# Input units of the first block in a new order, as filling of the recurrent chain and of attention; one activation table for exp and ln in the second block

## What is computed

```python
def first_block(x, ...):                 # per layer
    p_swa, p_rwkv, p_fox, p_dsa, p_gate = split_cols(x @ w_in, IN_GROUPS)
    o = swa_branch(...), rwkv7_branch(...), fox_branch(...), dsa_branch(...)
    gates = sigmoid(p_gate.reshape(B, S, 4, 1024) + gate_bias)
    x = layer_norm(DN_ALPHA * x + (sum_i gates[i] * (o[i] @ w_rows[i])) @ w_out, ...)
    x = layer_norm(DN_ALPHA * x + (swiglu(x) if layer == 0 else moe_ffn(x)), ...)
```

## Time and profile before

| | before |
|---|---|
| median of 3 runs | 2380.99 us (2380.73 to 2382.38) |
| the profiled execution | 2379.34 us, its span 2377.6 us |
| PE / DVE / ACT / POOL busy | 2177.4 / 654.0 / 435.2 / 81.7 us |
| mean granted clock of PE | 0.954 |
| read from HBM | 417.90 MB, 176 GB/s over the span |

### The profile page before, as it was taken

The page is one execution under the profiler, slowest core; times in us unless marked ns, Lnnn a source line. Parts: engine busy times, 40 slices in busy tenths (PEclk is TensorE's granted clock), DMA queues, the critical chain, the costliest instruction groups (busy, mean ns, idle before and its releaser), DMA issues.

```text
span 2377.6 us, 34188 instructions
## 1 busy us (share of the span) xinstructions
PE 2177.4 (92%) x14812; PEld 1566.2 (66%) x14812; DVE 654.0 (28%) x1567; ACT 435.2 (18%) x897; POOL 81.7 (3%) x180
## 2 busy tenths in 40 slices
PE   8999679999989897788899999988899998889998
PEld 7878457677768686565554365367577766757775
DVE  0051643424320333643200000033433332341001
ACT  0031131100010121230000000046610004661000
POOL 2000000001000000001000000000001010000000
PEclk9999869999999899788899999999999999999999
DMA  8333203488744232112899999953368854232442
GB/s 252 110 107 108 98 18 115 160 265 292 251 148 138 89 107 98 53 63 91 265 345 333 360 346 310 375 185 104 110 209 269 296 185 135 91 105 91 159 159 88
DMA packets 329659, 421.25 MB, mean 177 GB/s; under 512 B 21015, under 2 KB 277989, under 8 KB 329509
## 3 DMA queue, kind: packets, MB, share of 16 engines
q1 hardware_dynamic: 308304, 352.96, 46.0%
q0 software_dynamic: 13408, 50.66, 6.3%
q10 hardware_dynamic: 7796, 15.43, 1.9%
HBM read 417.90 MB, written 1.05 MB: 176 GB/s over the span
## 4 chain that ended last, share of the span: by engine, by line
PE 46%; ACT 4%; DVE 4%; issue 1%; DMA 1%; ACTq 0%; DVEq 0%
PE psum L1219 11%; PE psum L1336 10%; PE psum L1237 6%; PE psum L1396 5%; PE psum L1226 5%; PE psum L1635 2%; PE psum L1878 1%; PE psum L1255 1%; PE psum L1464 1%; PE psum L1325 1%; PE psum L1409 1%; ACT arena L996 1%; PE psum L1155 1%; ACT L967 1%; PE psum L1618 1%
## 5 line engine op out<-in xcount | busy, mean ns | idle before, releaser
L1219 PE MATMUL psum<-xT,ring 128*128 128x256 f32 (+1 forms) x3584 | 801.4, 384 | 7.0 <-DVEq L417 2.9
L1219 PEld LDWEIGHTS psum<-xT,ring 128*128 128x128 f32 (+1 forms) x3584 | 678.5, 190 | 129.5 <-issue 23.0
L1237 PE MATMUL psum<-ring,arena 128*128 128x512 f32 x528 | 232.2, 593 | 0.0
L1226 PE MATMUL psum<-ring,xT 128*128 128x256 f32 (+3 forms) x1024 | 216.8, 370 | 15.5 <-DVE arena L2268 8.1
L1226 PEld LDWEIGHTS psum<-ring,xT 128*128 128x128 f32 x1024 | 185.7, 199 | 44.6 <-DVE arena L2268 9.3
L1237 PEld LDWEIGHTS psum<-ring,arena 128*128 128x128 f32 x528 | 100.0, 190 | 114.2 <-issue 111.9
L2063 DVE TENSOR_TENSOR arena<-arena,psum 128x512 f32<-128x512 f32 x33 | 22.7, 688 | 410.7 <-PE psum L1219 235.0
L2052 DVE SCALAR_TENSOR_TENSOR arena<-arena,cond 128x256 f32<-128x256 f32 x336 | 135.0, 480 | 0.0
L1336 PE MATMUL psum<-ring,arena 128*32 128x256 f32 x2304 | 126.8, 379 | 0.7 <-DVE arena L2135 0.7
L657 ACT ACTIVATE arena<-psum 128x512 f32<-128x512 f32 x33 | 19.7, 597 | 578.2 <-PE psum L1219 571.9
L1336 PEld LDWEIGHTS psum<-ring,arena 128*32 128x32 f32 x2304 | 74.7, 110 | 51.2 <-issue 3.4
(11 more groups left out here) (392 smaller groups left out, 1972.8 us busy)
## 6 DMA issues: line engine op xcount, KB each, us to landing
ring<-in_w_in SPq DMA_DIRECT2D x80, 1024.0 KB, 5.3
ring<-in_exp_w SPq DMA_DIRECT2D x312, 256.0 KB, 6.1
arena<-in_w_mod POOLq DMA_DIRECT2D x48, 1024.0 KB, 9.4
ring<-in_ffn_w SPq DMA_DIRECT2D x33, 1024.0 KB, 6.8
arena<-in_exp_w SPq DMA_DIRECT2D x120, 256.0 KB, 7.1
ring<-in_w_gate SPq DMA_DIRECT2D x22, 1024.0 KB, 7.6
ring<-in_w_up SPq DMA_DIRECT2D x22, 1024.0 KB, 10.0
ring<-in_w_down SPq DMA_DIRECT2D x22, 1024.0 KB, 5.1
```

The lines of the kernel that those rows point to most:

```text
L1219: ins = pe.matmul(dst, w[:, k * 256 + c0:k * 256 + c0 + m], act_t[:, k, :], start=(k == 0), stop=(k == KT - 1))
L1226: ins = pe.matmul(dst, act_t[:, k, t * P:t * P + P], w[:, k * 256 + c0:k * 256 + c0 + n], start=(k == 0), stop=(k == KT - 1))
L1237: ins = pe.matmul(psum[:, 4 + 2 * t + h, :], gT[:, s % 3, f * 256 + t * P:f * 256 + t * P + P], w2[:, f * D + h * 512:f * D + h * 512 + 51 ...
```

## The change

The units of a layer are loaded and multiplied in the order 3, 4, 5, 6 (`RWKV_IN`), then 10, 11, 12, 7, 8, 9, 0, 1, 2 (`FILL_IN`), then the gates. Only the first four are done ahead of the chain, into banks 4, 5, 0 and 1. The other nine and the 16 gates are one list of 25 fills, handed out by `fill` at the places where `gates` stood and at some more: three (layer 1: two) before the up-projections instead of two, one behind the variance matmul, five (six) instead of two with the picking, five instead of one in attention. ACT copies all of them. Unit 11 is packed anew, so that one channel tile gives both kinds of keys and one token tile per half the values, the index weights and the forget logits, which two transposes turn later. The barrier behind the input stage is gone; DVE waits for the parameters and for ACT's copy of unit 5 by themselves. `load_params` waits for unit 5 in slot 2 where it waited for unit 2, the same third load. In the second block one table set that holds exp and ln is loaded ahead of its use in each layer, and each root gets a Newton step of three small DVE operations (`newton`).

```diff
+RWKV_IN = (3, 4, 5, 6)
+FILL_IN = (10, 11, 12, 7, 8, 9, 0, 1, 2)
+FILLS = len(FILL_IN) + 16
...
-        def in_bank(i):
-            return (4 + i) % 8
-
-        def in_copied(ready, l, i):
-            return ready("act" if i in (0, 1, 3, 5, 7, 9, 10) else "dve", "in", l, i)
+        RAW_BANK = {3: 4, 4: 5, 5: 0, 6: 1}
+        PAR_BANK = 2
...
-                for i, c in enumerate(units1):
+                for i in RWKV_IN + FILL_IN:
+                    c = units1[i]
                     if c is None:
-                        yield ("in", l, i), [(0, 128, w[:, :, IN_DSA + 256:IN_DSA + 384]),
-                                             (128, 68, w[:, :, IN_DSA + 640:IN_DSA + 708]),
+                        yield ("in", l, i), [(0, 64, w[:, :, IN_DSA + 256:IN_DSA + 320]),
+                                             (64, 64, w[:, :, IN_DSA + 640:IN_DSA + 704]),
+                                             (128, 64, w[:, :, IN_DSA + 320:IN_DSA + 384]),
+                                             (192, 4, w[:, :, IN_DSA + 704:IN_DSA + 708]),
...
+            def fill(l, n, banks):
 
                 for _ in range(n):
-                    j = gates_done[0] % 16
-                    gates_done[0] += 1
-                    cp, b = gate_place(j)
-                    act.wait_ge(*ready("pe_job", "gate", l, j))
-                    for i in range(2):
-                        c = 2 * cp + i
-                        step(act.activation(zb[:, b, c, :], psum[:, banks[j % len(banks)], i * 256:i * 256 + 256],
-                                            ACT.Identity, bias=prm(l, "gate_b", b * KT + c)), "zb", l, j)
-
-            gates_done = [0]
+                    j = filled[0] % FILLS
+                    filled[0] += 1
+                    bank = psum[:, banks[j % len(banks)], :]
+                    act.wait_ge(*ready("pe_job", "fill", l, j))
+                    if j >= len(FILL_IN):
+                        cp, b = gate_place(j - len(FILL_IN))
+                        for i in range(2):
+                            c = 2 * cp + i
+                            step(act.activation(zb[:, b, c, :], bank[:, i * 256:i * 256 + 256],
+                                                ACT.Identity, bias=prm(l, "gate_b", b * KT + c)), "filled", l, j)
...
+                    elif FILL_IN[j] == 2:
+                        for g in range(2):
+                            for h in range(2):
+                                step(act.copy(swa_k[hb(h), g, :], bank[hb(g), 0:256]))
+                        step(act.copy(swa_v[:], two(bank[:, 256:512])), "filled", l, j)
+                    elif FILL_IN[j] == 11:
+                        for h in range(2):
+                            step(act.copy(dsa_k[hb(h), :], bank[0:HD, 0:256]))
+                            step(act.copy(dsa_ki[hb(h), :], bank[HD:P, 0:256]))
+                        token = bank[:, 256:400].rearrange("p (t c) -> p t c", t=NT)
+                        step(act.copy(dsa_v[:], token[:, :, 0:HD]))
+                        step(act.activation(dsa_wi[:], token[:, :, HD:HD + 4], ACT.Copy, scale=SCALE * 0.5))
+                        step(act.copy(forget, token[:, :, HD + 4:HD + 8]), "filled", l, j)
+                    else:
+                        dst = {0: swa_q[:, 0:2, :], 1: swa_q[:, 2:4, :], 7: fox_q, 8: fox_k, 9: fox_v,
+                               10: dsa_q, 12: dsa_qi}[FILL_IN[j]]
+                        step(act.copy(dst[:], two(bank)), "filled", l, j)
...
-                act.wait_ge(*ready("slot2", "unit", "in", 0, 2))
+                act.wait_ge(*ready("slot2", "unit", "in", 0, 5))
...
-                for i, dst in ((0, swa_q[:, 0:2, :]), (1, swa_q[:, 2:4, :]), (3, raw[:, 0:2, 1:]),
-                               (5, raw[:, 4:6, 1:]), (7, fox_q[:]), (9, fox_v[:]), (10, dsa_q[:])):
+                for i, dst in ((3, raw[:, 0:2, 1:]), (5, raw[:, 4:6, 1:])):
                     act.wait_ge(*ready("pe_job", "in", l, i))
-                    step(act.copy(dst, psum[:, in_bank(i), :].rearrange("p (a b) -> p a b", a=2)), "in", l, i)
+                    step(act.copy(dst, two(psum[:, RAW_BANK[i], :])), "in", l, i)
+                fill(l, 1, (6,))
...
+                act.preload_act_table_set("natural_log_exp_and_others")
...
+            def fill(l, n, banks):
 
                 for _ in range(n):
-                    j = gates_done[0] % 16
-                    gates_done[0] += 1
+                    j = filled[0] % FILLS
+                    filled[0] += 1
                     bank = banks[j % len(banks)]
-                    if bank in gate_in:
-
-                        pe.wait_ge(*ready("act", "zb", l, gate_in[bank]))
-                    w = unit("gate", l, *gate_place(j))
-                    for i in range(2):
-                        ins = channel_tile(psum[:, bank, i * 256:i * 256 + 256], w, i * P, P)
-                    job(ins, "gate", l, j)
-                    used("gate", l, *gate_place(j))
-                    gate_in[bank] = j
-
-            gates_done, gate_in = [0], {}
+                    if bank in fill_in:
+                        pe.wait_ge(*ready("act", "filled", l, fill_in[bank]))
+                    key = ("in", l, FILL_IN[j]) if j < len(FILL_IN) else ("gate", l, *gate_place(j - len(FILL_IN)))
+                    w = unit(*key)
+                    if key == ("in", l, 9):
+                        for t in range(NT):
+                            ins = token_tile(psum[:, bank, t * 256:t * 256 + 256], w, 0, 256, t)
+                    elif key in (("in", l, 2), ("in", l, 11)):
+                        n_tok = P if key[2] == 2 else HD + 8
+                        channel_tile(psum[:, bank, 0:256], w, 0, P)
+                        for t in range(NT):
+                            ins = token_tile(psum[:, bank, 256 + t * n_tok:256 + (t + 1) * n_tok], w, P, n_tok, t)
+                    else:
+                        for i in range(2):
+                            ins = channel_tile(psum[:, bank, i * 256:i * 256 + 256], w, i * P, P)
+                    job(ins, "fill", l, j)
+                    used(*key)
+                    fill_in[bank] = j
+
+            filled, fill_in = [0], {}
...
+                for i in RWKV_IN[2:4]:
...
+                fill_in.clear()
+                fill(l, 1, (6,))
                 if l == 0:
-                    pe.wait_ge(*in_copied(ready, l, 6))
                     pe.wait_ge(S.sem("param"), N_PARAM_LOADS * 16)
                     for i in range(DEPTH):
-                        ins = pe.transpose(psum[:, in_bank(14), i * P:i * P + N_PAR], par_rows[0:N_PAR, i, :],
+                        ins = pe.transpose(psum[:, PAR_BANK, i * P:i * P + N_PAR], par_rows[0:N_PAR, i, :],
                                            ident[0:N_PAR, 0:N_PAR])
                     job(ins, "par")
                 else:
-                    pe.wait_ge(*in_copied(ready, l, 6))
-                    turn_mod(0, in_bank(14))
-                barrier()
-
-
-                gate_in.clear()
-                gates(l, G[0], (6,))
+                    turn_mod(0, PAR_BANK)
+                fill(l, G[0][l] - 1, (6,))
                 pe.wait_ge(*ready("act", "tanh", l))
...
                 pe.wait_ge(*ready("dve", "y_sq", l))
                 ins = pe.matmul(psum[:, 5, :], block_ones[:], sq[:], start=True, stop=True)
                 job(ins, "var", l)
-                gates(l, G[9], (6,))
+                fill(l, G[9], (6,))
                 barrier()
 
-                gate_in.clear()
+                fill_in.clear()
+                for t in range(NT):
+                    ins = pe.transpose(psum[0:4, 2, t * P:t * P + P], forget[:, t, :], ident[:])
+                job(ins, "forget", l)
...
-                gates(l, G[6], (0, 1))
+                fill(l, in_attention(l), (0, 1))
...
+            def newton(r, s, scale, add):
+
+                t = refine[:, 0:s.shape[1]]
+                step(dve.scalar_tensor_tensor(out=t, in0=r, scalar=-0.5 * scale, in1=r, op0=ALU.mult, op1=ALU.mult))
+                step(dve.scalar_tensor_tensor(out=t, in0=s, scalar=add, in1=t, op0=ALU.add, op1=ALU.mult))
+                step(dve.scalar_tensor_tensor(out=r, in0=t, scalar=1.5, in1=r, op0=ALU.add, op1=ALU.mult))
...
+                newton(ri8[:, b], ss8[:, b], 1.0, RMS_EPS)
...
+                newton(ro4[:, b, 0:m], os4[:, b, 0:m], 1.0 / d, 0.0)
...
-                for i in (2, 4, 6, 8, 11, 12, 13):
...
+                for i in (4, 6):
                     dve.wait_ge(*ready("pe_job", "in", l, i))
...
-                if l == 1:
-                    mod_columns(0, in_bank(14))
-                barrier()
+                    step(dve.tensor_copy(raw[:, i - 2 if i == 4 else i:(i - 2 if i == 4 else i) + 2, 1:],
+                                         two(psum[:, RAW_BANK[i], :])), "in", l, i)
+                if l == 0:
+                    dve.wait_ge(*ready("pool", "constants"))
+                    dve.wait_ge(*ready("act", "par"))
```

(21 more changed lines are left out.)

109 lines of the change are left out of this document (30 added, 79 removed).

## The result

The changed kernel takes 2264.25 us (median of 4 runs, 2261.19 to 2265.9) against 2381.68 us (4 runs, 2380.73 to 2383.3) of the kernel before on the same chip. The ratio is 0.9505, with a 95% interval of 0.9488 to 0.9521: 117.4 us or 4.9% less. The forecast was 2264.4. Its profiled execution took 2262.99 us, with a span of 2261.3, so the span is 116.3 us shorter.

The account below looks back on a forecast made before the run. PE bounds the kernel, busy 2177.4 of 2377.6 us. Gains of 42.8 (layer 0), 49.8 (layer 1) and 24 (second block), 116.6, leave a span of 2261.0; with 1.74 and 1.65 added, 2264.4 us, own range 2252 to 2280.

Parts of the forecast that it names:

- Unit 11: Input stage: its narrow pieces, together 21.3 us, become 7.2 when packed anew, saving 14.1 us per layer.
- Up to the chain: Start to up-projection: layer 0's at 67.4, 70.2 us earlier; layer 1's at 730.5 instead of 811.92, 81.4 earlier.
- Variance to index: Behind the variance matmul: one more fill, ACT's copy and the barrier take 9.4 us where 7.4 were.
- Attention: First scores to last weighing: 80 us; its end comes 42.8 us earlier in layer 0, 49.8 in layer 1.
- The fills behind the fox matmuls: Attention rounds 4 and 5: each fill takes 8.6 us, coming out of the low clock.
- The tail: Remaining rounds of attention behind round 5's fill: 19 us instead of 24.8, two rounds finding their data ready.
- After attention nothing changes: Between attention and the second block: no change in time, put at nothing.
- Second block: Table loads at roots go, Newton steps come: waits shrink by 19.9 us, the clock adds 4, together 24 us.
- Rival 1: Attention: low clock stays with the interleaved rounds, 10 us per layer, second block's 4 go: 2288 us; chance 0.17.
- Rival 2: Fox matmuls stay at full clock, 6 us per layer; second block loses all waits, 5.9: 2247 us; chance 0.12.
- Rival 3: Second block: combined table not used, 24 us not gained, Newton costs 0.6 at some ten roots: 2294; chance 0.06.
- Rival 4: Chain: PE's clock falls, fills take 14.1 us each; slower than before, 2405 us with 20 of them; chance 0.02.

Follow-up runs that it names:

- the second part alone: Kernel before with only the second block's edits, one exp/ln table set and the Newton steps: 2359.62 us, ratio 0.99.
- the second profiled execution: The changed kernel measured once more, nothing edited, on the same chip: 2265.47 us, ratio 0.9514 against the kernel before.

## Why the prediction was right, step by step

**Unit 11.** Foretold 14.1 us per layer; alone it gave 28.9 for two. Its 32 records of 72 columns take 3.69 (3.7 was taken). Its pieces of 256 and 16 bytes, priced at nothing, cost nothing that shows in the ring: behind 15 us PE has no wait for a slot of the first block.

**Up to the chain.** Layer 0's up-projection came at 66.34, foretold 67.4; the wait for ACT's copies is 2.06 (2.1), the parameters' DMA cost 0.37 (none, at most 2). That the fill behind this wait may run at the low clock was not in the sum; in six other profiled executions it did, which cost 1.4 to 3.0 us. In layer 1, 679.45 to 811.92 were 132.5 us from the first units to the up-projection, and 640.09 to 691.21 are 51.1: 81.4 less, as foretold, with the wait for the tanh at 3.78 (3.8).

**Variance to index.** The 9.4 of the forecast count from the end of the variance matmul; from there it is 8.2 us in both layers (9.3 from its start). The fill there hides 7.1 us of work per layer: taking it away cost 23.2 us in all, of which 17.8 have this cause in the rows and the rest is the clock in other places.

**Attention.** DVE has picked by 222.3, 9.0 us before PE's first scores, so it waits for PE as foretold. From the first scores on, layer 0 took 81.3 us and layer 1 78.4; I had 80. Right as a sum, with three sizes off in it. The fills behind the fox matmuls were put at 8.6 from one row; they took 10.21 and 9.88 in layer 0, 8.86 and 8.70 in layer 1, and in the second profiled execution 8.62 and 10.09, 8.86 and 8.73. The tail took 19.6 (19). Against these stands round 5, whose fox matmuls took 6.1 us in layer 0 where 7.5 was put, and in layer 1 round 4's, 5.5 where 7.3 was put: the clock fell later in them, or not before the fill. Layer 1's chain, from the up-projection to the index, took 128.5 where 132.1 was put. Of this 1.2 is the fill and the barrier behind the variance, and 2.0 a fill that came at the low clock in the kernel before, order of time on PE, layer 1, and now takes 7.19:

```profile
815.51 9.18 PE L1219 MATMUL psum<-xT,ring 128*128 128x256 f32 x32
```

So layer 0 gained 44.8 (42.8) and layer 1, counted from its own start, 55.2 (49.8).

**Given back between the layers.** "After attention nothing changes" is the step of the prediction that failed, a term put at nothing. Of the 44.8 us only 39.4 are left at layer 1's first units. 2.0 went at the branch products; 1.7 of that is the clock, low at the row's start: it took 36.49 us in both profiled executions of the changed kernel, and 34.80 in the kernel before and in most of the experiments. The other 3.4 went at the last modulation unit, order of time on PE:

```profile
615.43 2.57 PE L1198 MATMUL psum<-arena,ones 128*1 128x256 f32 x32 [2.97 <-DVE arena L2057]
617.93 8.12 PE L1269 MATMUL psum<-ring,arena 128*128 128x512 f32 x16
```

Before, the same two rows were:

```profile
656.42 1.91 PE L1175 MATMUL psum<-arena,ones 128*1 128x256 f32 x32 [1.17 <-DVE arena L2052]
658.26 7.13 PE L1237 MATMUL psum<-ring,arena 128*128 128x512 f32 x16
```

So the wait grew by 1.8 us, and the low clock behind it cost 1.65 (2.57 for 1.91, 8.12 for 7.13). DVE waits for the last 1 MB of the modulation weights, 10.59 us now and 8.79 before, though the transfer is asked for at the same distance from DVE's unit before it. The wait is 1.31 in the kernel with the second part alone, and 2.7 to 3.2 in every kernel that has unit 11 packed anew, the one with that alone included. It goes with the packing or with the earlier arrival that comes of it, and these runs do not tell which; why the transfer lands later stays open.

**Second block.** 22.2 us in the rows (layer 0 8.0, layer 1 14.2), 21.9 alone, 24 foretold. PE's waits fell by 16.9 us (19.9 foretold): the 2.2 that was to remain of the 4.36 is 2.21, but the 6.96 left 4.41 and not 3.7, the 0.59 stayed in both layers, and 0.38 and 0.37 are left of the two 1.70. The other 5.3 us are rows that got shorter (4 foretold for the clock). They did not where the forecast looked, as the unit behind the long wait still takes 9.67 us. The largest is behind the 4.36 of layer 1: to the next wait PE took 15.7 us at a clock of 0.73 (2050.29 to 2066.01) and now takes 13.3 at 0.87 (1942.43 to 1955.68).

**Balance.** 44.8 + 55.2 + 22.2 - 5.4 = 116.8, against 116.3 us of span; 0.5 more went elsewhere. The forecast met the time because layer 1's 5.4 us more stood against 5.4 given back; single terms were off by 2 to 5 us, the changed kernel's own executions lie between 2261.2 and 2269.4, and an agreement to 0.2 us is luck.

**The rivals.** Rival 1, the low clock that stays in the interleaved rounds, did not come: rounds 1 to 3 ran at the full clock (fills of 7.17). The low clock was where the forecast had it, in the fox rounds, and its fills cost 2.9 us more than put there in layer 0 and 0.4 in layer 1. Rival 2's full clock in the fox rounds did not come. Rival 3 fell with the kernel that has the second part alone. Rival 4 did not show: the fills of the chain took 7.1 to 7.2 us.

## What to carry to other kernels

Where an engine waits for others at some places and has solid work at others, find out of the solid work what nobody needs yet and move it into the waits; it is nearly free as long as the wait is longer than the filling (0.3 us for a fill of 7.1 here), and the wait's low clock goes with it. Then count the filling on both sides: at the picking five units outlasted the 28 us they covered, and in the tail two of them cover 8 us per layer. Give two fills in a row two banks, so that the second need not wait for the copy of the first. Before moving work, look at what makes it expensive by itself: nearly a third of the first block's gain came from one unit's narrow matmuls.

## What the runs showed of the hardware

The clock fell in the fox rounds without any wait of PE. In layer 0 of the kernel after the fox matmuls run from 258.26 on, with no gap in the rows, and at 261.90 the same form of row takes 0.63 us that took 0.38 before. What PE did before it fell was matmuls with four rows between others with 64. The first full fill behind them took 8.6 to 10.2 us instead of 7.17, and not the same from one execution of a kernel to the next (10.21 and 8.62 at the same place). With the fills split the clock still fell in three of the four rounds. Why the clock fell there is not shown; that the four-row matmuls bring it down is what the rows suggest, and no run took them out.

The cost of a short wait also differs from one execution to the next. Behind the same wait of 2.06 us the same fill took 7.17 us in three profiled executions and 8.55 to 10.20 in six.

A table load took 1.283 us at every root, and its activation followed 0.02 us behind it. The 64 loads were 82 us of ACT, and without them the kernel is 22 us faster, as PE waited behind some of the roots only.
